# Seven products of quarter blocks in cross-attention's query and output projections

## The chip, the cores and the metric

The kernel runs on one core of a Trainium2 chip. The metric is the device time of one execution in microseconds (us); the median of the runs is what counts. A profiled execution gives the trace.

## What is computed

A decoder trunk of two layers over 256 tokens of width 1024, float32 throughout. Each layer mixes tokens, attends to 256 memory tokens, and applies a mixture of sixteen experts. The change is in the cross-attention:

```python
def memory_cross_attention(h, mem_n, wq, wkv, wo):
    q = (h @ wq).reshape(B, S, X_HEADS, X_DH)
    k, v = jnp.split(mem_n @ wkv, 2, axis=-1)
    ...
    s = jnp.einsum('bshd,bmhd->bhsm', q, k).astype(F32) * (X_DH ** -0.5)
    p = jax.nn.softmax(s, axis=-1)
    o = jnp.einsum('bhsm,bmhd->bshd', p, v.astype(F32)).reshape(B, S, D)
    return o.astype(h.dtype) @ wo

for l in range(DEPTH):
    ...
    x = x + jnp.concatenate([y_hg, y_att], axis=-1) @ w_out[l]
    x = x + memory_cross_attention(rms_norm(x, norm_cross[l]), rms_norm(mem, norm_mem[l]),
                                   wq_x[l], wkv_x[l], wo_x[l])
    x = x + hierarchical_moe(rms_norm(x, norm_ffn[l]), ...)
```

h is 256x1024, wq and wo are 1024x1024.

## The kernel before

**Engines and queues.** The kernel is written engine by engine, each engine's instructions in the order of the code, with semaphores between them. The sync engine (SP) only issues loads. TensorE does all products and transposes, VectorE and ScalarE empty PSUM and do the sums, maxima and exponentials, GpSimd does small roots and, in the token mixing, weight sums.

**Weights.** They come in units of 2 MB (128 partitions x 4096 floats, "ring" in the trace), each as two loads of 1 MB. The ring has six slots. `unit_places` deals units to slots in a fixed round: the layer's mixing units in the order of `UNITS` (o0 and o1: projection of the mixed tokens, q0 and q1: query projection, p0 and p1: output projection of cross-attention), a slot "sums" without a load, and then 48 expert units, six for each of eight pairs of experts: two gate, two up, two down. SP issues them in this order and waits before each until the slot's former tenant was used for the last time (`LAST_USE`, by the name of the job). In the last layer three more slots open for the experts, in buffers that have come free: `LATE`, `KEYS` and `WORK`, at the places of `LAST_SLOTS`.

**Banks.** Every product that goes to PSUM is a job with a name. `job_list` gives the order, and "A" or "D" says whether ScalarE or VectorE empties it; `bank_plan` deals the eight banks. TensorE opens a job when the bank's former job has been emptied (`open_bank`), and `wait_emptied` and `wait_job` are waits for the one or the other.

**Seven products.** The token mixing already computes two of its 256x1024x1024 projections together from seven products of quarter blocks (`seventh`, jobs m1 to m7, L617): the tokens are halved by rows and by columns, the weights likewise, and sums and differences of blocks are formed first. `rows_block(m, k)` is a quarter of the normed, transposed tokens hT (tokens m, columns k), `weight_block` half a unit, `token_sums(i)` a quarter of xs that holds a sum.

**Cross-attention before.** The products of the mixed tokens, wo00, wo10, wo01, wo11 (L710, closed by `rows_out`), are added to x by VectorE (L1577, in `add_rows`). Then for each tile m of 128 tokens ScalarE squares and sums x (L1034), GpSimd takes the root (L1225, L1226), VectorE scales x into xs (L1417), TensorE transposes xs (L508, jobs t3_m0 and t3_m1), and VectorE copies into hT with the gains (L1427). The query projection makes the queries transposed, weights stationary: qx0 in two halves of 128 tokens (L762), so that it can begin with the first tile, qx1 to qx3 over 256 tokens (L528 in `project_T`). ScalarE copies them to QxT (in "rot", L1056). `memory_scores` (L775) makes four jobs sx00, sx01, sx10, sx11, heads 2g and 2g+1 of tile m; VectorE takes maxima (L1589), ScalarE the exponentials (L1131), VectorE divides (L1597). The shares are transposed (pt jobs, L508), copied (L1602), and multiplied with the memory values (L791, jobs px0 to px3), which go back to hT. The output projection is four jobs ox00, ox10, ox01, ox11 of 128 tokens x 512 columns with the tokens stationary (L710), eight matmuls each, first half of the contraction first; VectorE adds them to x (L1577). Then come norm, transposes (t5 jobs), the router (L822) and the experts (L882 gate and up, L936 down).

Of the kernel before, what the change touches and what calls it, by code (L numbers as in the profile page):

```python
# [8 lines left out]
P = 128  # L9
# [7 lines left out]
D = 1024  # L17
# [21 lines left out]
LAST_SLOTS = {0: LATE, 5: KEYS, 6: WORK}  # L39
UNITS = ["k0", "k1", "v0", "v1", "hf", "hq", "hi", "av", "hg", "aq", "ak", "o0", "o1", "q0", "q1", "p0", "p1"]  # L40
SUMS = "sums"
# [10 lines left out]
def job_list():  # L52
# [15 lines left out]
    jobs += [(f"t3_{m}{c}", "D") for m, c in quarters]  # L68
    jobs += [(f"qx{k}", "A") for k in range(4)]
    jobs += [(f"sx{g}{m}", "A") for g in range(2) for m in range(M)]  # L70
    jobs += [(f"pt0{jb}", "D") for jb in range(2)] + [("px0", "D"), ("px1", "A")]
    jobs += [(f"pt1{jb}", "D") for jb in range(2)] + [("px2", "D"), ("px3", "A")]
    jobs += [(f"ox{n}{m}", "D") for m in range(M) for n in range(2)]
# [12 lines left out]
OPENED_AT = {"wo00": "et0", "wo10": "et0", "wo01": "et2", "wo11": "et2", "ox00": "px2", "ox10": "ox00", "ox01": "ox00", "ox11": "ox00"}  # L86


def bank_plan(more):
# [8 lines left out]
    for name in NAMES + more:  # L98
        for early, at in OPENED_AT.items():
            if at == name:  # L100
                begin(early)
        if name in more:
            free.sort(key=lambda bank: bank[0] in FIRST_ROWS)
        if name not in begun:
            begin(name)
        free.append((bank_of[name], name))
# [6 lines left out]
            "o0": "wo01", "o1": "wo11", "q0": "qx1", "q1": "qx3", "p0": "ox01", "p1": "ox11"}  # L113


def unit_places():
# [4 lines left out]
    for layer in range(DEPTH):  # L121
        units = UNITS[KV_UNITS if layer else 0:]
        at_sums = units.index("av") + 1
        order += [(layer, name, None) for name in units[:at_sums] + [SUMS] + units[at_sums:]]
# [4 lines left out]
    for layer, key, slot in order:  # L129
# [3 lines left out]
        places[layer, key] = slot, sum(k != SUMS for _, k in had) + 1, had[-1] if had else None  # L133
# [6 lines left out]
SCORES = [(0, (0, 2, 4, 6)), (0, (1, 3, 5, 7)), (1, (0, 2)), (1, (1, 3)), (1, (4, 6)), (1, (5, 7))]  # L140

# [42 lines left out]
def trunk(nc, x_in, mem_in, pos_in, inv_in, gains_in, og_in, w_mix, w_router, w_experts, nf_in, out):  # L184
    ctx = ExitStack()
    with ctx:
# [92 lines left out]
        token_sum, weight_sum = sem("token_sum"), sem("weight_sum")  # L279
        q_done = sem("q_done")  # L280
# [107 lines left out]
        def weight_block(L, name, k):  # L388
            return unit(name, L)[:, 4 * k:4 * k + 4, :]

# [97 lines left out]
        def _(pe):  # L488
# [79 lines left out]
            def layers_from(L, sums_read=None):  # L568
# [181 lines left out]
                w = unit("q0", L)  # L750
                for m in range(M):
# [3 lines left out]
                    if m == 0:  # L755
                        wait_unit(L, "q0")
                        b = open_bank(L, "qx0")
                    for k in range(2):
                        for c in range(C):
                            if k == 0 and c % 4 == 0:  # L760
                                wait_emptied(pe, L, f"t3_{m}{c // 4}")
                            last = nc.tensor.matmul(b[:, k * T + m * P:k * T + (m + 1) * P], w[:, c, k * P:(k + 1) * P],  # L762
                                                    hT[:, c, m * P:(m + 1) * P], start=(c == 0), stop=(c == C - 1))
                close(last)
                for k in range(1, 4):
                    wait_unit(L, f"q{k // 2}")
                    project_T(L, f"qx{k}", hT, unit(f"q{k // 2}", L), 2 * (k % 2))
                wait_emptied(pe, L, "qx3")
                def memory_scores(g):
                    for m in range(M):  # L770
                        b = open_bank(L, f"sx{g}{m}")
                        for i in range(2):
                            h = 2 * g + i
                            for k in range(2):
                                last = nc.tensor.matmul(b[:, i * T:(i + 1) * T], QxT[:, 2 * h + k, m * P:(m + 1) * P],  # L775
                                                        KT[:, 2 * h + k, :], start=(k == 0), stop=(k == 1))
# [1040 lines left out]
```

## Time and profile before

| | us |
|---|---|
| median of 3 runs | 1061.05 |
| lowest and highest | 1060.15, 1063.64 |
| span of the profiled execution | 1058.3 |
| TensorE busy in it | 1020.7 (96%) |
| VectorE busy | 413.4 (39%) |
| ScalarE busy | 135.6 (13%) |
| GpSimd busy | 98.2 (9%) |

The span reaches from the first to the last instruction of the profiled execution. Busy times are sums over the whole span; which engine is waited for in a stretch is read from the chain of waits and the timeline. A float32 matmul stands as two MATMUL rows in the trace, and its weight load as two LDWEIGHTS rows, which run beside matmuls. A row's mean duration is from its start to its modelled end, and rows overlap; the busy time divided by the count gives the distance at which they follow each other.

### The profile page before, as it was taken

How to read it: one execution, taken by the hardware profiler on the slowest of the kernel's cores; microseconds unless marked ns; L12 is line 12 of the kernel's file. 1: busy time of each engine (PE TensorE's matmuls, PEld its weight loads, DVE VectorE, ACT ScalarE, POOL GpSimd, SP SyncE). 2: the span in 40 equal slices, each digit the busy share in tenths (PEclk: the TensorE clock that was granted, in tenths of full speed). 3: DMA queues.
4: the chain of work that ended last, by engine and by line, in shares of the span. 5: the costliest groups of instructions: out<-in, count | busy, mean ns of one | idle time of the engine just before them, and what ended most of it. 6: DMA issues, size and time to landing. Idle time of an engine off the chain costs nothing.

```text
span 1058.3 us, 10640 instructions
## 1 busy us (share of the span) xinstructions
PE 1020.7 (96%) x4360; PEld 546.8 (52%) x4360; DVE 413.4 (39%) x734; ACT 135.6 (13%) x307; POOL 98.2 (9%) x123
## 2 busy tenths in 40 slices
PE   6999999999999999999999999999999999999996
PEld 6667556567564453333334855566864433333332
DVE  3433474622143324232334526572032534433333
ACT  2211001412010011110111000041011010011011
POOL 2051131000001000000000512200000100000000
PEclk9999999999999999999999999999999999999999
DMA  9944002954049999999999420088364699999994
GB/s 359 424 183 159 1 0 100 412 207 159 1 159 355 381 423 422 414 423 420 420 421 420 180 80 0 1 356 346 120 234 159 241 423 420 421 420 421 422 421 169
DMA packets 43671, 293.54 MB, mean 277 GB/s; under 512 B 5344, under 2 KB 5600, under 8 KB 10848
## 3 DMA queue, kind: packets, MB, share of 16 engines
q1 hardware_dynamic: 36848, 266.35, 61.8%
q10 hardware_dynamic: 5616, 22.24, 5.4%
q0 software_dynamic: 1152, 4.19, 1.0%
q8 instruction: 37, 0.61, 0.2%
q14 instruction: 18, 0.15, 0.0%
HBM read 283.33 MB, written 9.44 MB: 277 GB/s over the span
## 4 chain that ended last, share of the span: by engine, by line
PE 89%; DVE 3%; DMA 3%; ACT 2%; SPq 2%; issue 1%; POOL 0%; DVEq 0%; POOLq 0%; ACTq 0%
PE bank L882 19%; PE bank L710 10%; PE bank L936 10%; PE bank L528 9%; PE bank L518 8%; PE bank L546 5%; PE bank L548 5%; PE bank L941 5%; PE bank L617 5%; PE bank L639 3%; DMA ring<-in_w_experts 3%; PE bank L508 2%; SPq L469 2%; PE bank L762 1%; PE bank L775 1%; PE bank L791 1%
## 5 line engine op out<-in xcount | busy, mean ns | idle before, releaser
L882 PE MATMUL bank<-ring,hT 128*64 128x512 f32 x704 | 182.8, 594 | 0.5 <-DMA ring<-in_w_experts 0.5
L710 PE MATMUL bank<-ring,hT 128*128 128x512 f32 x256 | 112.1, 594 | 0.0
L882 PEld LDWEIGHTS bank<-ring,hT 128*64 128x64 f32 x704 | 57.8, 137 | 94.2 <-issue 92.8
L1721 DVE TENSOR_TENSOR x<-bank,x 128x512 f32<-128x512 f32 x64 | 44.3, 692 | 138.1 <-PE bank L941 138.1
L528 PE MATMUL bank<-hT,ring 128*128 128x256 f32 x448 | 97.4, 379 | 0.8 <-DVE hT L1427 0.8
L528 PEld LDWEIGHTS bank<-hT,ring 128*128 128x128 f32 x448 | 84.9, 190 | 12.8 <-issue 1.4
L518 PE MATMUL bank<-ring,hT 128*128 128x512 f32 x192 | 84.4, 592 | 0.0
L710 PEld LDWEIGHTS bank<-ring,hT 128*128 128x128 f32 x256 | 48.0, 190 | 57.7 <-issue 56.8
L936 PE MATMUL bank<-ring,Vx 128*64 128x512 f32 x208 | 58.3, 596 | 2.7 <-ACT Vx L1163 2.4
L941 PE MATMUL bank<-PT 128*128 128x512 f32 x128 | 59.2, 605 | 0.0
L936 PE MATMUL bank<-ring,work 128*64 128x512 f32 x256 | 56.7, 595 | 2.4 <-ACT work L1163 2.4
L518 PEld LDWEIGHTS bank<-ring,hT 128*128 128x128 f32 x192 | 35.6, 190 | 40.2 <-issue 40.2
L1221 POOL TENSOR_TENSOR sm<-sm 128x1 f32<-128x1 f32 x4 | 1.0, 239 | 474.5 <-ACT rot L1043 474.5
L941 PEld LDWEIGHTS bank<-PT 128*128 128x128 f32 x128 | 23.0, 189 | 36.0 <-issue 35.0
L936 PEld LDWEIGHTS bank<-ring,work 128*64 128x64 f32 x256 | 17.6, 137 | 36.3 <-issue 32.0
L882 PE MATMUL bank<-late,hT 128*64 128x512 f32 x80 | 35.3, 594 | 0.5 <-DMA late<-in_w_experts 0.5
L936 PEld LDWEIGHTS bank<-ring,Vx 128*64 128x64 f32 x208 | 18.2, 137 | 33.4 <-issue 26.6
L882 PE MATMUL bank<-work,hT 128*64 128x512 f32 x80 | 35.3, 594 | 0.0
L639 PEld LDWEIGHTS bank<-work 128*128 128x128 f32 x256 | 31.1, 192 | 7.7 <-issue 6.7
L1577 DVE TENSOR_TENSOR x<-bank,x 128x512 f32<-128x512 f32 x16 | 11.0, 690 | 59.5 <-PE bank L710 59.5
L1709 DVE TENSOR_SCALAR work<-work 128x512 f32<-128x512 f32 x8 | 3.4, 427 | 78.4 <-ACT work L1159 78.4
L1169 ACT ACTIVATE PT<-bank 128x512 f32<-128x512 f32 x32 | 19.1, 597 | 108.5 <-PE bank L936 108.5
(270 smaller groups left out, 1287.3 us busy)
## 6 DMA issues: line engine op xcount, KB each, us to landing
ring<-in_w_experts SPq DMA_DIRECT2D x160, 1024.0 KB, 14.3
ring<-in_w_mix SPq DMA_DIRECT2D x60, 1024.0 KB, 16.8
late<-in_w_experts SPq DMA_DIRECT2D x12, 1024.0 KB, 21.5
keys<-in_w_experts SPq DMA_DIRECT2D x10, 1024.0 KB, 21.0
work<-in_w_experts SPq DMA_DIRECT2D x10, 1024.0 KB, 24.8
late<-in_w_mix ACTq DMA_DIRECT2D x4, 2048.0 KB, 10.2
rot<-by_slot ACTq DMA_DIRECT2D x14, 512.0 KB, 8.2
by_slot<-late ACTq DMA_DIRECT2D x1, 4096.0 KB, 37.9
```

Source lines behind the costliest of these rows:

```text
L469: sp.dma_start(slot_view(slot)[:, half * n:(half + 1) * n], src[:, half * n:(half + 1) * n]).then_inc(loaded[slot][half], 16)
L518: last = nc.tensor.matmul(b[:, :], lhs[:, c, m * P:(m + 1) * P], w[:, c, :], start=(c == 0), stop=(c == C - 1))
L528: last = nc.tensor.matmul(b[:, k * T:(k + 1) * T], w[:, c, (n2 + k) * P:(n2 + k + 1) * P], rhs[:, c, :], start=(c == 0), stop=(c == C - 1))
L546: last = nc.tensor.matmul(b[:, k * T:(k + 1) * T], w[:, c, n:n + P], memory[:, c, :], start=(c == 0), stop=(c == C - 1))
L548: last = nc.tensor.matmul(b[:, :], memory[:, c, (j % 2) * P:(j % 2 + 1) * P], w[:, c, :], start=(c == 0), stop=(c == C - 1))
L617: last = nc.tensor.matmul(b[:, :], rows_at[:, c, :], weights[:, c, :], start=(c == 0), stop=(c == 3))
L639: last = nc.tensor.matmul(b[:, a * P:(a + 1) * P], K[:, a, m * P:(m + 1) * P], Q[:, a, m * P:(m + 1) * P], start=True, stop=True)
L710: last = nc.tensor.matmul(held[name[1:], n, m][:, :], hT[:, c, m * P:(m + 1) * P], w[:, c, :], start=(c == 0), stop=(c == C - 1))
L882: last = nc.tensor.matmul(banks[2 + g][b2 * CAP:(b2 + 1) * CAP, :], rows_T_of(p)[:, c, b2 * CAP:(b2 + 1) * CAP], w, start=(c == 0), stop=( ...
L936: last = nc.tensor.matmul(banks[5 + n][b2 * CAP:(b2 + 1) * CAP, :], ractT_of[L][:, c, b2 * CAP:(b2 + 1) * CAP], w, start=(c == 0), stop=(c ...
L941: routed_job(nc.tensor.matmul(banks[OUT_BANK[n][m]][:, :], gatedT[:, m, :], yrows[:, n * W:(n + 1) * W], start=True, stop=True))
L1721: V.tensor_tensor(xv, banks[OUT_BANK[n][m]][:, :], xv, ALU.add).then_inc(r_added[L], 1)
```

## The change

Both projections of cross-attention are computed from seven products of quarter blocks, as the token mixing's are.

- **Query projection.** `q_seventh` replaces L762 and the three jobs of L528. A product is 128 tokens x 512 query columns over 512 of the contraction: sixteen matmuls of 128 columns with the weights stationary. Their order is q_1, q_2, q_6, q_5, q_7, q_3, then two score jobs, then q_4, then two score jobs. Four of the seven products accumulate on a bank that already holds another product's sum (`ONTO`): q_6 on q_1, q_7 on q_6, q_4 on q_7, q_3 on q_5. The bank is read after each product that is part of a result, and the next product waits for that read. ScalarE copies q_1, q_6, q_5 and q_4 into QxT; VectorE adds q_2, q_7 and q_3 there. Results: block (tile 0, columns 1) is q_1 + q_2, (0, 0) is q_1 + q_6 and q_5 + q_3, and so on.
- **Output projection.** `p_seventh` replaces the four ox jobs: p_1, then the values of heads 2 and 3, then p_7, p_6, p_5, p_4, p_2, p_3, four matmuls of 512 columns each, with p_6 on p_1, p_4 on p_7 and p_3 on p_5. VectorE adds the banks into x, p_6's into three blocks.
- **Sums.** VectorE forms four weight sums of 128x2048 and four token sums of 128x512 for each projection. The weight sums stand in new slots of the ring (`Q_SUMS` after q1, `P_SUMS` after p1) and in place in the first halves of q0, q1, p0 and p1. VectorE waits for all of q0 and q1 before its first add into x, and for all of p0 and p1 after the add of q_2.
- **Slots.** The two new tenants move all later units by one or two slots; `LAST_SLOTS` opens the last layer's three slots one unit earlier. p1 now follows o0 in its slot.
- **Order of the scores.** Tile 1 of heads 0 and 1 comes first (`SX_ORDER`).

The diff, cut to its core:

```diff
-LAST_SLOTS = {0: LATE, 5: KEYS, 6: WORK}
+LAST_SLOTS = {0: LATE, 4: KEYS, 5: WORK}
...
+SUMS_AFTER = {"av": SUMS, "q1": Q_SUMS, "p1": P_SUMS}
...
+ONTO = {"q_6": "q_1", "q_7": "q_6", "q_4": "q_7", "q_3": "q_5", "p_6": "p_1", "p_4": "p_7", "p_3": "p_5"}
...
-            "o0": "wo01", "o1": "wo11", "q0": "qx1", "q1": "qx3", "p0": "ox01", "p1": "ox11"}
+            "o0": "wo01", "o1": "wo11", "q0": "q_3", "q1": "q_4", Q_SUMS: "q_4", "p0": "p_2", "p1": "p_3", P_SUMS: "p_4"}
...
+                def q_seventh(name):
+
+                    rows_at, sums_at, weights, weights_at = {
+                        "q_1": (rows_block(0, 0), 0, weight_block(L, "q1", 0), 0), "q_2": (rows_block(0, 1), 0, weight_block(L, "q1", 1), 0),
+                        "q_5": (token_sums(0), 1, weight_block(L, Q_SUMS, 0), 1), "q_6": (token_sums(1), 2, weight_block(L, Q_SUMS, 1), 2),
+                        "q_7": (token_sums(2), 3, weight_block(L, "q0", 0), 3), "q_3": (token_sums(3), 4, weight_block(L, "q0", 1), 0),
+                        "q_4": (rows_block(1, 1), 0, weight_block(L, "q1", 0), 4)}[name]
...
+                    if sums_at:
+                        pe.wait_ge(q_token_sum, 4 * L + sums_at)
+                    if weights_at:
+                        pe.wait_ge(q_weight_sum, 4 * L + weights_at)
+                    b = open_bank(L, name)
+                    for n in range(4):
+                        for c in range(4):
+                            last = nc.tensor.matmul(b[:, n * P:(n + 1) * P], weights[:, c, n * P:(n + 1) * P], rows_at[:, c, :],
+                                                    start=(name not in ONTO and n == 0 and c == 0), stop=(n == 3 and c == 3), skip_group_check=(name in ONTO))
+                    close(last)
...
+                memory_scores(0, 1, "q_7")
+                memory_scores(0, 0, "q_3")
+                q_seventh("q_4")
+                memory_scores(1, 0, "q_2")
+                memory_scores(1, 1, "q_4")
...
+                    b = open_bank(L, name)
+                    for c in range(4):
+                        last = nc.tensor.matmul(b[:, :], rows_at[:, c, :], weights[:, c, :], start=(name not in ONTO and c == 0),
+                                                stop=(c == 3), skip_group_check=(name in ONTO))
+                    close(last)
+
+                p_seventh("p_1")
+                memory_values(1)
+                for i in (7, 6, 5, 4, 2, 3):
+                    p_seventh(f"p_{i}")
...
+                q_weights(1, qt1, q12, q11)
+                q_weights(2, qt2, q22, qt1)
+                add_out(0, 0)
+                q_weights(3, q12, q22, q12)
+                add_out(1, 0)
...
+                q_sum("q_2", 0, 1, "q_1")
+                q_weights(4, q11, q21, qt2)
...
+                p_weights(1, pt1, p12, p11)
+                p_weights(2, pt2, p22, pt1)
+                p_weights(3, p12, p22, p12)
+                q_sum("q_7", 1, 0, "q_5")
+                q_sum("q_3", 0, 0, "q_6")
...
+                p_sum("p_1", (1, 0))
...
+                p_sum("p_7", (0, 1))
+                p_weights(4, p11, p21, pt2)
...
+                p_sum("p_6", (0, 1), (0, 0), (1, 1))
...
+                p_sum("p_5", (0, 1))
+                p_sum("p_4", (0, 0))
...
+                p_sum("p_2", (1, 0))
+                p_sum("p_3", (1, 1))
```

TensorE in layer 0, from the transposes of the second tile to the end of the scores, before (L508 transposes, L762 and L528 query projection, L775 scores; an x16 row is sixteen matmuls):

```order
L508 MATMUL bank3<-ident,xs 128x128 x4
L508 MATMUL bank4<-ident,xs 128x128 x4
L762 MATMUL bank5<-hT,ring 128x128 x16
L528 MATMUL bank6<-hT,ring 128x256 x16
L528 MATMUL bank1<-hT,ring 128x256 x16
L528 MATMUL bank2<-hT,ring 128x256 x16
L775 MATMUL bank7<-keys,rot 128x256 x4
L775 MATMUL bank0<-keys,rot 128x256 x4
L775 MATMUL bank3<-keys,rot 128x256 x4
L775 MATMUL bank4<-keys,rot 128x256 x4
```

and after (L785 is `q_seventh`, L803 the scores; a product whose tokens are named xs takes a token sum):

```order
L526 MATMUL bank4<-ident,xs 128x128 x4
L526 MATMUL bank5<-ident,xs 128x128 x4
L785 MATMUL bank6<-hT,ring 128x128 x16
L785 MATMUL bank3<-xs,ring 128x128 x16
L785 MATMUL bank1<-xs,ring 128x128 x16
L785 MATMUL bank3<-xs,ring 128x128 x16
L785 MATMUL bank1<-xs,ring 128x128 x16
L803 MATMUL bank2<-keys,rot 128x256 x4
L803 MATMUL bank7<-keys,rot 128x256 x4
L785 MATMUL bank3<-hT,ring 128x128 x16
L803 MATMUL bank0<-keys,rot 128x256 x4
L803 MATMUL bank4<-keys,rot 128x256 x4
```

All matmuls of the query projection now have 128 columns, and the last product stands between the score jobs.

VectorE in layer 0 from its copy of the first attention values to its last copy into hT, before (L1569 the copy, L1577 adds into x, L1417 the norm's scaling, L1427 copies into hT):

```order
L1569 COPY hT<-bank3 128x512
L1577 TENSOR_TENSOR x<-bank5,x 128x512
L1577 TENSOR_TENSOR x<-bank6,x 128x512
L1417 TENSOR_SCALAR xs<-x,sm 128x1024
L1577 TENSOR_TENSOR x<-bank1,x 128x512
L1577 TENSOR_TENSOR x<-bank2,x 128x512
L1427 TENSOR_TENSOR hT<-bank7,gains 128x4x128
L1427 TENSOR_TENSOR hT<-bank0,gains 128x4x128
L1417 TENSOR_SCALAR xs<-x,sm 128x1024
L1427 TENSOR_TENSOR hT<-bank3,gains 128x4x128
L1427 TENSOR_TENSOR hT<-bank4,gains 128x4x128
L1589 TENSOR_REDUCE sm<-bank7 128x2
```

and after, in two pieces, around the adds into x (L1617 the copy, L1626 weight sums, L1647 adds, L1465 scaling):

```order
L1617 COPY hT<-bank3 128x512
L1626 TENSOR_TENSOR ring<-ring 128x2048 x2
L1647 TENSOR_TENSOR x<-bank5,x 128x512
L1626 TENSOR_TENSOR ring<-ring 128x2048
L1647 TENSOR_TENSOR x<-bank6,x 128x512
L1465 TENSOR_SCALAR xs<-x,sm 128x1024
L1647 TENSOR_TENSOR x<-bank1,x 128x512
```

and between the last copy into hT and the first maximum (L1636 token sums, L1675 adds of q_2, q_7 and q_3, L1631 weight sums of the output projection):

```order
L1475 TENSOR_TENSOR hT<-bank5,gains 128x4x128
L1636 TENSOR_TENSOR xs<-hT 128x512
L1636 TENSOR_TENSOR xs<-xs,hT 128x512
L1636 TENSOR_TENSOR xs<-hT 128x512
L1636 TENSOR_TENSOR xs<-hT,xs 128x512
L1675 TENSOR_TENSOR rot<-bank6,rot 128x4x128
L1626 TENSOR_TENSOR ring<-ring 128x2048
L1631 TENSOR_TENSOR ring<-ring 128x2048 x3
L1675 TENSOR_TENSOR rot<-bank3,rot 128x4x128
L1675 TENSOR_TENSOR rot<-bank1,rot 128x4x128
L1692 TENSOR_REDUCE sm<-bank2 128x2
```

Three weight sums now stand before and between the first adds, four token sums and four more weight sums between the last copy into hT and the first maximum.

## Rows read from the trace of the kernel before

**Rows 1.** The execution's span and mean granted clock.

```profile
core 0: 1058.3 us, clock 0.999
```

**Rows 2.** The span in 40 slices: granted clock and DMA, in tenths.

```profile
PEclk9999999999999999999999999999999999999999
DMA  9944002954049999999999420088364699999994
```

**Rows 3.** The chain of waits: start us, length us, what.

```profile
223.51 3.81 PE bank L762 x32
...
228.53 3.84 PE bank L762 x32
232.37 20.74 PE bank L528 x96
253.78 7.19 PE bank L775 x32
...
263.13 3.72 PE bank L791 x16
...
267.73 3.53 PE bank L710 x8
...
274.71 24.05 PE bank L710 x56
298.78 0.70 DVE x L1577
...
736.43 3.81 PE bank L762 x32
...
830.09 13.98 PE bank L882 x64
...
1014.87 27.22 DMA ring<-in_w_experts
```

**Rows 4.** Sync queue issues; one stretch: engines busy, clock, DMA share, GB/s.

```profile
177.21 8.09 SPq L469 DMA_DIRECT2D ring<-in_w_mix  x12
...
837.27 0.80 SPq L469 DMA_DIRECT2D late<-in_w_experts  x2
...
837.20:1042.10 204.90, 199.75 (x874) 72.51 (x870) 81.01 (x116) 20.98 (x38) 0.00 (x0) 1.00 1.00 416
```

**Rows 5.** L762 by form: count | busy us, mean ns; TensorE waits.

```profile
L762 PE MATMUL bank<-hT,ring 128*128 128x128 f32 x128 | 15.3, 278 | 2.1 <-DVE hT L1427 2.1
...
L762 PEld LDWEIGHTS bank<-hT,ring 128*128 128x128 f32 x128 | 14.6, 192 | 3.0 <-issue 1.9 <-DVE hT L1427 1.2
...
PE bank L762 <- DVE hT L1427: 2.1, 4, 0.7
...
PE bank L775 <- ACT rot L1056: 1.4, 2, 0.7
```

**Rows 6.** Sums on VectorE and GpSimd by form: count | busy us, mean ns.

```profile
L1545 DVE TENSOR_TENSOR work<-bank,bias 128x256 f32<-128x256 f32 x8 | 3.3, 417 | 0.0
...
L1439 DVE TENSOR_TENSOR xs<-hT 128x512 f32<-128x512 f32 x4 | 2.8, 692 | 0.1
...
L1261 POOL TENSOR_TENSOR ring<-ring 128x2048 f32<-128x2048 f32 x2 | 9.0, 4508 | 32.4 <-DMA ring<-in_w_mix 32.4
```

**Rows 7.** Timeline around layer 0's first adds into x: start us, length us.

```profile
206.71 0.69 DVE L1569 COPY hT<-bank 128x512 f32<-128x512 f32 x1 [1.24 <-PE bank L701]
...
215.07 0.69 DVE L1577 TENSOR_TENSOR x<-bank,x 128x512 f32<-128x512 f32 x1 [2.74 <-PE bank L710]
...
217.97 0.75 DVE L1417 TENSOR_SCALAR xs<-x,sm 128x1024 f32<-128x1024 f32 x1 [2.20 <-POOL sm L1226]
...
221.74 1.04 PE L508 MATMUL bank<-ident,xs 128*128 128x128 f32 x8
```

**Rows 8.** Timeline of VectorE and GpSimd in layer 0's first token sums.

```profile
70.99 4.89 DVE L1439 TENSOR_TENSOR xs<-xs,hT 128x512 f32<-128x512 f32 x1
...
70.40 4.93 POOL L1265 TENSOR_TENSOR ring<-ring 128x2048 f32<-128x2048 f32 x1
```

More of the change, by code:

```diff
@@ L67, in job_list @@
     jobs += [(f"wo{n}{m}", "D") for m in range(M) for n in range(2)]
-    jobs += [(f"t3_{m}{c}", "D") for m, c in quarters]
-    jobs += [(f"qx{k}", "A") for k in range(4)]
-    jobs += [(f"sx{g}{m}", "A") for g in range(2) for m in range(M)]
+    jobs += [("t3_00", "D"), ("t3_01", "D"), ("q_1", "A"), ("t3_10", "D"), ("t3_11", "D"), ("q_2", "D"), ("q_6", "A"), ("q_5", "A"), ("q_7", "D"), ("q_3", "D"), ("sx01", "A"), ("sx00", "A"),
+             ("q_4", "A"), ("sx10", "A"), ("sx11", "A")]
     jobs += [(f"pt0{jb}", "D") for jb in range(2)] + [("px0", "D"), ("px1", "A")]
-    jobs += [(f"pt1{jb}", "D") for jb in range(2)] + [("px2", "D"), ("px3", "A")]
-    jobs += [(f"ox{n}{m}", "D") for m in range(M) for n in range(2)]
+    jobs += [(f"pt1{jb}", "D") for jb in range(2)] + [("p_1", "D"), ("px2", "D"), ("px3", "A")]
+    jobs += [(f"p_{i}", "D") for i in (7, 6, 5, 4, 2, 3)]
     jobs += [(f"t5_{m}{c}", "D") for m, c in quarters]
@@ L85 @@
 FIRST_ROWS = (0, 1)
-OPENED_AT = {"wo00": "et0", "wo10": "et0", "wo01": "et2", "wo11": "et2", "ox00": "px2", "ox10": "ox00", "ox01": "ox00", "ox11": "ox00"}
+OPENED_AT = {"wo00": "et0", "wo10": "et0", "wo01": "et2", "wo11": "et2"}
+ONTO = {"q_6": "q_1", "q_7": "q_6", "q_4": "q_7", "q_3": "q_5", "p_6": "p_1", "p_4": "p_7", "p_3": "p_5"}
 def bank_plan(more):
@@ L103, in bank_plan @@
             free.sort(key=lambda bank: bank[0] in FIRST_ROWS)
-        if name not in begun:
+        if name in ONTO:
+            bank_of[name], before[name] = bank_of[ONTO[name]], ONTO[name]
+        elif name not in begun:
             begin(name)
-        free.append((bank_of[name], name))
+        if name not in ONTO.values():
+            free.append((bank_of[name], name))
     return bank_of, before
@@ L122, in unit_places @@
         units = UNITS[KV_UNITS if layer else 0:]
-        at_sums = units.index("av") + 1
-        order += [(layer, name, None) for name in units[:at_sums] + [SUMS] + units[at_sums:]]
+        for name in units:
+            order.append((layer, name, None))
+            if name in SUMS_AFTER:
+                order.append((layer, SUMS_AFTER[name], None))
         more = LAST_SLOTS if layer == DEPTH - 1 else {}
@@ L132, in unit_places @@
         had = tenants.setdefault(slot, [])
-        places[layer, key] = slot, sum(k != SUMS for _, k in had) + 1, had[-1] if had else None
+        places[layer, key] = slot, sum(k not in ALL_SUMS for _, k in had) + 1, had[-1] if had else None
         had.append((layer, key))
@@ L754, in layers_from, with memory_scores @@
                         transposes(L, f"t3_{m}{c2}", by_columns(xs, m, c2))
[L755 to L776, printed above, removed]
-                        close(last)
+                    q_seventh(f"q_{m + 1}")
+                for i in (6, 5, 7, 3):
+                    q_seventh(f"q_{i}")
+                def memory_scores(g, m, ready):
+                    wait_emptied(pe, L, ready)
+                    b = open_bank(L, f"sx{g}{m}")
+                    for i in range(2):
+                        h = 2 * g + i
+                        for k in range(2):
+                            last = nc.tensor.matmul(b[:, i * T:(i + 1) * T], QxT[:, 2 * h + k, m * P:(m + 1) * P],
+                                                    KT[:, 2 * h + k, :], start=(k == 0), stop=(k == 1))
+                    close(last)
                 def memory_weights(g):
```

152 lines of the change are left out of this document (110 added, 42 removed).

## The prediction

> **What bounds the kernel now.** First the span and the granted clock: one core, 1058.3 us, clock 0.999 [rows 1]. The median of the runs shown is 1061.05 us, so 2.75 us lie outside the span; I carry them unchanged and make the sum against the span. Then the slices [rows 2]: the granted clock is at its top level throughout (in tenths, 9 everywhere), so no term here is a clock term, and the DMA engines are full in two stretches, the expert phases, and nearly idle between them. Then the chain of waits [rows 3]. Through layer 0's cross-attention it is TensorE nearly without a break: L762 and L528 (query projection), L775 (scores), L791 (values), L710 (output projection). Layer 1 repeats it 512.92 us later (736.43 against 223.51). The last 44 us are different: 27.22 us of a load of expert weights, then a little TensorE.
>
> So what does a gain in cross-attention do to the end? Layer 0's experts are TensorE's work, and it starts earlier by the gain. In layer 1 the tail is the weight stream: from 837.2 to 1042.1 us the DMA engines are 1.00 busy at 416 GB/s [rows 4]. 39 units of 2.10 MB at that rate are 197 us, the rest are rows of tokens. The stretch starts when the sync queue can issue the first unit whose slot pair 0's gate products free: issued at 837.27, after the chain's gate products that begin at 830.09 [rows 3, 4]. Nine of the 48 expert units are loaded before that point, 39 after. The change moves more units into the ring, but LAST_SLOTS keeps it at nine: of layer 1's units, (1, 3) is still the first that waits for (0, 0). The stream thus starts earlier by whatever TensorE gains, and its length stays. A gain in either layer therefore reaches the end whole, unless one of the cases below holds.
>
> **The change, part by part, per layer.** A matmul of this kernel stands as two in the trace, so sixteen in the order are 32 rows. *Query projection, products.* Before: 64 rows of 128 columns, 3.81 + 3.84 us, and 96 rows of 256 columns, 20.74 us [rows 3], 28.39 us. After: seven products of sixteen matmuls of 128 columns, 224 rows. The 128-column pitch is 15.3 us / 128 = 0.1195 us [rows 5], 26.77 us. Gain 1.62 us: less than an eighth of the work, because 128 columns cost 0.1195 where half of a 256-column row is 0.108.
>
> *Query projection, waits.* Before, TensorE stood still 2.1 us at L762 and 1.4 us at L775 over both layers [rows 5]. The first train of L762 ends at 227.32, eight transpose rows take 0.88 us (266.85 to 267.73 in the chain), and the second starts at 228.53 [rows 3]: 0.33 us a layer is a wait for VectorE's copy of these transposes. In their place q_2 reads tokens copied earlier, and has no such wait. L775's 0.70 us a layer is the wait for the last projection's copy; the first scores now read products that were summed earlier. Gain 1.03 us, if the covers below hold. Laying the new order out from 223.51 us with the pitches above, q_1 ends at 227.3, q_2 at 232.0, q_6 235.8, q_5 239.6, q_7 243.5, q_3 247.3, two score tiles (7.19 / 4 = 1.80 each) 250.9, q_4 254.7, two more tiles 258.3. The values follow 2.16 us after the last score tile before (260.97 to 263.13) [rows 3], and still do: 260.5 instead of 263.13.
>
> *VectorE's new sums.* Eight weight sums of 128x2048 a layer. VectorE has no such row; bounds are its 128x512 row with both inputs in SBUF, 0.692 us, times four, 2.77 us, and GpSimd's 128x2048 row, 4.508 us [rows 6]; from below, the slope between 128x256 (0.417) and 128x512 is 0.275 us for 256 elements, so 0.692 + 6 x 0.275 = 2.34 us. I take 2.36 with its wait, the slope being VectorE's own. Eight token sums cost 0.73 each. Where each falls:
> - Three weight sums before and between the first adds into x. VectorE is free from about 207.4 (after the copy at 206.71); two sums end at 212.1, the add of wo00 (ready one product of 3.44 us before wo10) at 212.8, the third at 215.2, the add of wo10 starts at 215.2 against 215.07 now. The normed tile is then ready at about 218.9 and TensorE wants it at 221.74 [rows 7]. Cover 2.8 us; free. They need q0 and q1 loaded: six units are issued from 177.21, and at the 416 GB/s of the long stretch a unit of 2.10 MB takes 5.0 us [rows 4], so q1, fourth in line, lands at about 199. Layer 1 the same.
> - Four token sums after the last hT tile, 229.1 to 232.0. q_6 wants the second, at 230.6, at 232.0. Free.
> - Weight sum 4 and the three p sums, 232.8 to 242.3; then the add of q_7 (243.5), wanted at 247.3. Free with 3.0 us to spare. q_3's add ends 1.0 us before sx00 wants it, q_4's copy on ScalarE 1.1 us before sx11 does.
> - In the output part: token sums 2 and 3 wait for px3's copy, 272.7, and end at 274.2; p_6 wants the third at 275.4. The last weight sum, 276.2 to 278.6, is wanted by p_4 at 282.3. Free.
>
> *Output projection.* Before 64 rows of 512 columns: 3.53 + 24.05 = 27.58 us [rows 3], 0.43 each. After 56 rows: 24.13. Gain 3.44 us. p_1 waits for px0 and px1 as ox00 did. The tail is unchanged: tile 0's last add is p_4's, two products before the end as ox10's was, so the first norm has its squares, root and scale under p_2 and p_3; the second norm begins after p_3 as it did after ox11 (DVE at 298.78).
>
> *Loads.* p1 now waits for wo01; in layer 1 it holds the sync queue, and the first expert unit behind it, until about 731 (wo01 ends 3.4 us after wo10, 218.5 in layer 0); it lands at about 737, wanted at about 748. The last three units before gate 0 are issued in the last 4 us of the projection (p_2's unit and p_3's two) and need 15 us; gate 0 starts 18 us after its end (811.7 to 830.09). Free.
>
> *GpSimd's port.* Elsewhere the trace shows what a GpSimd sum does to VectorE: a 128x512 sum took 4.89 us instead of 0.69 beside a 4.93 us sum of GpSimd [rows 8]. In this stretch GpSimd has only the roots of the norms, and VectorE stands at a wait for each of them, so neither holds the other. Nothing counted.
>
> Sum per layer: 1.62 + 1.03 + 3.44 = 6.1 us; two layers 12.2 us. 1061.05 - 12.2 = **1048.8 us**.
>
> **Rivals.**
> - *The pace of 128 columns is the weight load's.* A load of 128x128 weights lasts 192 ns against the pitch of 119.5 [rows 5]. If 16 products in a row wore out the overlap, the query part would cost 224 x 0.192 = 43.0 us, 14.6 more than now: per layer 14.6 - 1.03 - 3.44 = 10.1 us slower, 1081 us. Against it: the 128 rows of L762 run in long trains of 32 at 119.5. Chance 0.02. The Trainium skill (TensorE: Matmul & The Clock Gate, "The mechanism") has a rule that points to this rival: a weight load runs beside matmuls only if it goes to another group of rows of the array. With its price for a load of 128 columns, 107 ns, set before each row of 0.108 us, an estimate by that page is 224 x 0.215 = 48.2 us for the query part. By that rule the trace disagrees: rows that fill all 128 rows of the array already follow at 119.5 ns, less than one load lasts.
> - *VectorE becomes the bound (the one that ends slower).* At a price d for a 128x2048 sum, the first norm is late by 3d - 9.5 us and q_7's add by 4d - 13.7 us, where these are positive. At GpSimd's 4.5 us that is 4.0 + 4.3 = 8.3 us lost against 6.1 won: 2.2 us slower a layer, 1065.5 us. It costs from d = 3.2 on and decides from d = 4.2. For it: GpSimd's row. Against: VectorE's 0.692 us. Chance 0.04.
> - *The weight stream hides layer 1's gain.* If the stream did not start earlier (a unit less before gate 0, or late landings), one layer's 6.1 us would be lost: 1054.9 us. For it: the chain's 27.22 us of DMA. Against: the stream starts with a release by TensorE. One unit of 2 MB fewer is 5.0 us, nearly the same. Chance 0.07.
> - *The change doesn't save what it says:* the covers of 1.0 and 1.1 us (q_3, q_4) and the waits at the banks shared by two products fail by about 1 us each: 1051 us. Chance 0.12.
>
> **How the numbers follow.** Forecast 0.75, with 1047.5 to 1050.5 of its own; the last rival 0.12, the stream 0.07, VectorE 0.04, the pace 0.02. From below, the shorter gaps between longer trains may give 1 us more. The range, 1047.0 to 1055.5, takes in all but the two slow rivals and odd cases. A measurement of this kernel can tell about 0.3%, 3.2 us, from no change: 1057.9 to 1064.2 is "the same". Faster 0.91, same 0.03, slower 0.06.
>
> **What would show it.** In the profile after: the query products' rows at a pitch of 119 to 121 ns, 224 a layer; no idle time before the scores' rows; VectorE's 128x2048 rows at 2.3 us; 56 rows of 512 columns in the output projection without a gap; layer 1's first gate product at about 818 instead of 830.09; the weight stream starting at about 825 and still some 205 us long. Wrong if the 128-column pitch is above 0.13, if a VectorE weight sum takes over 3.2 us, if TensorE stands before the score tiles, or if the stream still starts where it did.

## The result, and the profile after

The changed kernel takes 1044.31 us, the median of 4 runs (1044.12 to 1045.82), against 1061.58 us for the kernel before in 4 runs beside it (1060.15 to 1063.64): a ratio of 0.983, with a 95% interval of 0.981 to 0.985. It is faster, as predicted, but by 17.3 us, not 12.2; 1044.3 lies below the range of 1047.0 to 1055.5. The profiled executions say nearly the same, 16.4 us: a span of 1041.9 us against 1058.3, at a mean granted clock of 0.998 against 0.999.

```profile
core 0: 1041.9 us, clock 0.998
```

```profile
PEclk9999999999999999999999999999999999999999
DMA  9954001844169999999999520074385899999994
```

As in [rows 2], the clock is at its top level throughout, and the DMA engines are full in the two expert phases. The chain of waits through layer 0's cross-attention, and its end (start us, length us, what), which answers to [rows 3]:

```profile
223.19 3.81 PE bank L785 x32
227.00 0.87 PE bank L526 x8
227.87 17.87 PE bank L785 x160
245.74 3.46 PE bank L803 x16
249.19 3.57 PE bank L785 x32
252.76 3.47 PE bank L803 x16
...
258.40 3.72 PE bank L819 x16
...
263.01 3.67 PE bank L849 x8
...
270.13 20.61 PE bank L849 x48
290.77 0.70 DVE x L1732
...
814.32 13.98 PE bank L929 x64
...
998.35 27.32 DMA ring<-in_w_experts
```

L785 is the query product, L526 the transposes, L803 the scores, L819 the values, L849 the output product, L1732 the last add into x, L929 an expert's gate product; the last row is the load of the last expert weights. From the first query row to the end of the scores TensorE has no gap (the six rows add up to 33.05 of 33.04 us); before it had 1.00 us of them. By stretches, in us:

| stretch, layer 0 | before | after | gained | predicted |
|---|---|---|---|---|
| start of the last train of wo to the first query row | 15.54 | 15.36 | 0.18 | 0 |
| first query row to the end of the scores | 37.46 | 33.04 | 4.42 | 2.65 |
| end of the scores to the first value row | 2.16 | 2.17 | 0 | 0 |
| first value row to the last add into x | 35.65 | 32.37 | 3.28 | 3.44 |
| sum | 90.81 | 82.94 | 7.87 | 6.1 |

The last row, twice, is 15.7 us, and layer 1's first gate product moves from 830.09 to 814.32, by 15.77. The weight stream, one window, against [rows 4]:

```profile
821.50:1025.70 204.20, 199.29 (x874) 72.15 (x870) 80.97 (x116) 20.93 (x38) 0.00 (x0) 1.00 1.01 416
```

Its first load is issued at 821.49, 15.78 us earlier than the 837.27 of before, and it is 204.2 us long instead of 204.9. The two profiles then differ by 16.4 us; the 0.9 us that the medians differ by beyond that most likely lie in how executions start (below); only profiled executions show that. The query rows by form, the new sums of VectorE, and what TensorE still waits for (count | busy us, mean ns | idle; then us in total, times, longest):

```profile
L785 PE MATMUL bank<-xs,ring 128*128 128x128 f32 x256 | 28.9, 275 | 0.0
...
L1631 DVE TENSOR_TENSOR ring<-ring 128x2048 f32<-128x2048 f32 x8 | 18.3, 2289 | 0.2
L1626 DVE TENSOR_TENSOR ring<-ring 128x2048 f32<-128x2048 f32 x8 | 18.3, 2283 | 0.1
L803 PE MATMUL bank<-keys,rot 128*128 128x256 f32 x64 | 14.5, 379 | 0.0
...
PE bank L819 <- DVE PT L1705: 2.6, 2, 1.3
```

28.9 / 256 is 0.113 us a row where the prediction had 0.1195. The sums cost VectorE 2.28 us (predicted 2.34 before its wait). L775's wait of [rows 5] has gone, L803 has none.

### The profile page after: what moved, and what is told of

It reads as the page before. It is cut to its first block, busy times and chain, and to the rows that moved or that the text cites. A ratio compares the mean times of both kernels' runs of the same rounds, so it can differ in the third digit from the quotient of the medians.

```text
span 1041.9 us, 10960 instructions
## 1 busy us (share of the span) xinstructions
PE 1006.3 (97%) x4472; PEld 543.1 (52%) x4472; DVE 470.3 (45%) x782; ACT 135.7 (13%) x307; POOL 98.5 (9%) x123
## 4 chain that ended last, share of the span: by engine, by line
PE 89%; DVE 3%; DMA 3%; SPq 1%; ACT 1%; issue 1%; POOL 0%; DVEq 0%; POOLq 0%; ACTq 0%
PE bank L929 19%; PE bank L983 10%; PE bank L536 8%; PE bank L564 5%; PE bank L728 5%; PE bank L546 5%; PE bank L566 5%; PE bank L988 5%; PE bank L785 5%; PE bank L849 5%; PE bank L635 5%; PE bank L657 3%; DMA ring<-in_w_experts 3%; PE bank L526 2%; SPq L487 1%; PE bank L819 1%
## 5 line engine op out<-in xcount | busy, mean ns | idle before, releaser
L929 PE MATMUL bank<-ring,hT 128*64 128x512 f32 x752 | 196.6, 594 | 0.2 <-DMA ring<-in_w_experts 0.2
L929 PEld LDWEIGHTS bank<-ring,hT 128*64 128x64 f32 x752 | 62.3, 137 | 108.2 <-issue 107.0
L1856 DVE TENSOR_TENSOR x<-bank,x 128x512 f32<-128x512 f32 x64 | 44.3, 692 | 137.7 <-PE bank L988 137.7
L536 PE MATMUL bank<-ring,hT 128*128 128x512 f32 x192 | 84.4, 592 | 0.0
L536 PEld LDWEIGHTS bank<-ring,hT 128*128 128x128 f32 x192 | 35.6, 190 | 40.2 <-issue 40.2
L546 PE MATMUL bank<-hT,ring 128*128 128x256 f32 x256 | 55.7, 379 | 0.8 <-DVE hT L1475 0.8
L728 PE MATMUL bank<-ring,hT 128*128 128x512 f32 x128 | 56.3, 596 | 0.0
L546 PEld LDWEIGHTS bank<-hT,ring 128*128 128x128 f32 x256 | 48.6, 190 | 8.0 <-issue 1.4
L728 PEld LDWEIGHTS bank<-ring,hT 128*128 128x128 f32 x128 | 23.8, 190 | 28.7 <-issue 28.1
L983 PE MATMUL bank<-ring,Vx 128*64 128x512 f32 x160 | 36.5, 596 | 2.0 <-ACT Vx L1211 1.7
L929 PE MATMUL bank<-late,hT 128*64 128x512 f32 x80 | 35.3, 594 | 0.5 <-DMA late<-in_w_experts 0.5
L1331 POOL TENSOR_TENSOR work<-work 128x256 f32<-128x256 f32 x28 | 20.6, 735 | 121.1 <-PE bank L657 121.0
L657 PE MATMUL bank<-work 128*128 128x128 f32 x256 | 31.2, 275 | 0.0
L1475 DVE TENSOR_TENSOR hT<-bank,gains 128x512 f32<-128x512 f32 x24 | 15.3, 683 | 34.1 <-PE bank L526 34.1
```

Source lines behind the costliest of these rows:

```text
L536: last = nc.tensor.matmul(b[:, :], lhs[:, c, m * P:(m + 1) * P], w[:, c, :], start=(c == 0), stop=(c == C - 1))
L546: last = nc.tensor.matmul(b[:, k * T:(k + 1) * T], w[:, c, (n2 + k) * P:(n2 + k + 1) * P], rhs[:, c, :], start=(c == 0), stop=(c == C - 1))
L657: last = nc.tensor.matmul(b[:, a * P:(a + 1) * P], K[:, a, m * P:(m + 1) * P], Q[:, a, m * P:(m + 1) * P], start=True, stop=True)
L728: last = nc.tensor.matmul(held[name[1:], n, m][:, :], hT[:, c, m * P:(m + 1) * P], w[:, c, :], start=(c == 0), stop=(c == C - 1))
L929: last = nc.tensor.matmul(banks[2 + g][b2 * CAP:(b2 + 1) * CAP, :], rows_T_of(p)[:, c, b2 * CAP:(b2 + 1) * CAP], w, start=(c == 0), stop=( ...
L983: last = nc.tensor.matmul(banks[5 + n][b2 * CAP:(b2 + 1) * CAP, :], ractT_of[L][:, c, b2 * CAP:(b2 + 1) * CAP], w, start=(c == 0), stop=(c ...
```

## What the extra gain could be

The prediction missed 1.8 us a layer between the first query row and the values. Two readings stand against each other.

**A, the train.** The chain shows how rows of 128 columns follow each other when nothing breaks the train: 17.87 / 160 = 0.1117 us. A train of 32 that starts after a pause lasts 3.81 = 0.347 + 31 x 0.1117: its first row counts with its whole length (the longest of the query rows in the profile is 0.348 us, the middle one 0.275), 0.24 us more than a row inside a train; the train of 32 that follows the scores directly lasts 3.57 = 32 x 0.1117. All four trains of [rows 5] start after a pause, so 15.3 / 128 = 0.1195 holds a quarter of a microsecond of restart in every 32 rows. By A the change gains 28.39 - (3.81 + 17.87 + 3.57) = 3.14 us in the query products, and 0.26 more because the scores no longer start after a pause (7.19 against 3.46 + 3.47).

**B, the wait.** The 128-column row does cost 0.1195 us, or as much more as its weight load (192 ns) shows through, and the gain beyond 2.65 us comes from elsewhere in the change: a wait or a contention that the profile of before does not name, or the output projection.

## The experiments

Times of whole executions also differ by how they start: the first load of the memory tokens and the first train of TensorE vary by 2 to 3 us between executions of one kernel. Two chain rows, of the changed kernel's profile and of a repeat of it, show where TensorE's second train begins:

```profile
39.67 27.47 PE bank L566 x64
```

```profile
42.56 27.47 PE bank L566 x64
```

Besides the times the table therefore gives the profiled span less the start of this row ("rest"), in us; before it is 1018.5, and three profiles of the changed kernel give 1002.2, 1002.3 and 1002.5.

| run | median us (runs) | ratio, 95% interval | rest | against after's 1002.2 |
|---|---|---|---|---|
| e1 query part only | 1052.44 (4) | 0.992 [0.990, 0.993] | 1009.1 | +6.9 |
| e2 output part only | 1055.39 (4) | 0.994 [0.993, 0.996] | 1011.1 | +8.9 |
| e3 before, short rows | 1061.89 (10) | 1.000 [0.999, 1.002] | 1019.6 | (before +1.1) |
| e4 doubled sums | 1075.10 (4) | 1.011 [1.009, 1.014] | 1031.0 | +28.8 |
| e5 a slot less | 1050.73 (4) | 0.990 [0.988, 0.992] | 1007.6 | +5.3 |
| e6 after again | 1046.43 (5) | 0.986 [0.984, 0.987] | 1002.3 | +0.1 |
| e7 shares early | 1043.67 (5) | 0.983 [0.981, 0.984] | 999.3 | -2.9 |
| e8 wait first | 1046.31 (1) | | 1002.3 | +0.1 |
| e9 one sum more | 1045.80 (5) | 0.984 [0.982, 0.985] | 1002.7 | +0.4 |
| e10 two sums more | 1049.19 (6) | 0.988 [0.986, 0.990] | 1006.3 | +4.1 |
| e11 after, third time | 1046.57 (4) | 0.984 [0.982, 0.986] | 1002.5 | +0.3 |

### The halves of the change: e1 and e2

e1 keeps the query part alone, e2 the output part alone, each cut out of the changed kernel. From e1's edit:

```diff
-LAST_SLOTS = {0: LATE, 4: KEYS, 5: WORK}
+LAST_SLOTS = {0: LATE, 5: KEYS, 6: WORK}
...
-SUMS_AFTER = {"av": SUMS, "q1": Q_SUMS, "p1": P_SUMS}
...
+SUMS_AFTER = {"av": SUMS, "q1": Q_SUMS}
...
-                p_seventh("p_1")
...
+                for n, m in outputs:
+                    close(rows_out("pox", n, m, range(4, C)))
```

> The query projection by seven products, the output projection as before. Theory A (the prediction's pitch was too high: the steady distance of 128-column rows is 0.1117 us, and a train that stands alone shows its last row's full length besides, so fewer breaks are worth more): 4.4 us a layer in the stretch from the first query product to the last maximum, and 0.15 us from the copies that now stand ahead of a wait, 9.1 us in all, ratio 0.9914. Theory B (the prediction's 0.1195 us and waits as counted): 2.65 us a layer, 5.3 us in all, ratio 0.9950. Theory C (the gain comes from the output projection or from the two together): under 5 us, and less than the whole minus the other half.

> The output projection by seven products, the query projection as before. All theories but C: eight rows of 512 columns fewer a layer, 3.3 to 3.4 us, 6.6 to 6.9 us in all, ratio 0.9936. Theory A with the sum: the gains of this kernel and of the one with the query part alone add up to the whole change's 17.3 us less about 1 us. Theory C: over 8 us here.

Against before the rest shrinks by 9.4 us in e1 and by 7.4 in e2, 16.8 together where the whole change has 16.3, so nothing of note comes from the two together. The predicted shares were 5.3 and 6.9 us. Up to layer 1's first gate product, before the weight stream has a part in it, the gains are 9.2 us in e1, 6.7 in e2 and 15.6 in the whole change (its start again counted from TensorE's second train). The miss is in the query part. e1's chain has the same rows as the whole change's:

```profile
223.41 3.81 PE bank L785 x32
227.22 0.87 PE bank L526 x8
228.09 17.87 PE bank L785 x160
```

This speaks for A, and rules the output projection out as a source.

### The pace alone: e3

The kernel before, with qx1 to qx3 as twice as many rows of 128 columns; the work and the order of all else are the same.

```diff
-                    project_T(L, f"qx{k}", hT, unit(f"q{k // 2}", L), 2 * (k % 2))
+                    project_T_short(L, f"qx{k}", hT, unit(f"q{k // 2}", L), 2 * (k % 2))
...
+                for m in range(M):
+                    for k in range(2):
+                        for c in range(C):
+                            last = nc.tensor.matmul(b[:, k * T + m * P:k * T + (m + 1) * P], w[:, c, (n2 + k) * P:(n2 + k + 1) * P],
+                                                    rhs[:, c, m * P:(m + 1) * P], start=(c == 0), stop=(c == C - 1))
```

> The kernel before, with the 96 rows of 256 columns of the query projection (qx1 to qx3) issued as 192 rows of 128 columns in one unbroken train, weights loaded twice; nothing else differs. Theory A: 192 x 0.1117 = 21.45 us in place of 20.74, 0.7 us a layer slower, 1.4 us in all, ratio 1.0013. Theory B: 192 x 0.1195 = 22.94 us, 2.2 us a layer, 4.4 us in all, ratio 1.0042. The rival by the weight load's 0.192 us: 36.9 us, 16 us a layer, 32 us in all, ratio 1.030.

The train, where before had `20.74 PE bank L528 x96` [rows 3], and the loads in it (both layers):

```profile
232.65 21.45 PE bank L539 x192
```

```profile
L539 PE MATMUL bank<-hT,ring 128*128 128x128 f32 x384 | 43.2, 275 | 0.0
L539 PEld LDWEIGHTS bank<-hT,ring 128*128 128x128 f32 x384 | 43.0, 192 | 0.0
```

21.45 / 192 = 0.1117 us, in a kernel that has nothing else of the change: 0.71 us a layer more than 96 rows of 256 columns, where 0.1195 would have made it 2.2. The rest grew by 1.1 us, the ratio is 1.000. B's pace falls. So does the prediction's rival of the weight load: 192 loads of 192 ns each stand in the 21.45 us, and the rows don't slow to the loads' length. The 0.71 us, 3.7 ns for each row of 128 columns, is all that twice as many rows and loads cost; no run tells the two apart. The Trainium skill (TensorE: Matmul & The Clock Gate, "Step-by-step: what each phase is for") says that in a stream the drain of one matmul hides behind the next and that only a lone one pays for it; by that rule, the trace agrees: 0.24 us more for a row after a pause, none inside a train.

### VectorE's covers: e9, e10 and e4

A cover is the time by which VectorE has something ready before TensorE wants it. e9 puts one more weight sum ahead of the three before the first adds into x, e10 two, and e4 doubles seven of the eight weight sums of a layer. The added sums change no result: each is overwritten by a later sum, or (two of e4's) forms again what stands there already.

```diff
+                more_weights(qt1, q12, q11)
                 q_weights(1, qt1, q12, q11)
+                more_weights(qt2, q22, qt1)
                 q_weights(2, qt2, q22, qt1)
```

The first line is e9, both are e10; e4 has such a line ahead of seven `q_weights` and `p_weights`.

> One more weight sum of 128x2048 (2.3 us; its result is overwritten) ahead of the three that stand before the first adds into x, in both layers. Cover theory (the prediction's): in the changed kernel the first normed tile is ready at 218.65 and TensorE wants it at 221.76, and the add of wo10 has some 0.3 us between it and the sum before; 2.3 us more on VectorE still fit. Time as the changed kernel of the same call, within 0.5 us; no wait for VectorE's L1465 before TensorE's L526. Rival (VectorE's chain is already the bound there, the three sums cost time): 2.3 us more a layer, 4.6 us.

> Two more such sums, 4.6 us a layer. Cover theory: the cover of about 3.1 us is overrun by 1.3 to 1.5 us (the run with three more showed a wait of 3.7 us for 6.9 us of sums, a cover of 3.2): 2.6 to 3.0 us slower than the changed kernel of the same call. The granted clock: the run with all sums doubled showed it at its lower level after waits of 3.7 and 6 us of TensorE. If it falls after a wait of 1.4 us too, the next transposes and the train of q_1 last longer (up to 0.87 and 3.57 us more), and the loss is up to 6 us more over two layers; if it does not fall, these show 0.87 and 3.81 us as ever.

> The changed kernel with seven of VectorE's eight weight sums a layer preceded by one more of the same size (their results are overwritten or not used), 4.6 us for a pair. The prediction's formula at d = 4.61, with the cover of q_7's add 1.5 us shorter because the products are faster: 4.3 + 6.2 = 10.5 us a layer against the changed kernel; laid out on its timeline 4.1 us late at q_1 and 6.0 us at the first score tile, 10.1 us a layer. So about 1064.5 us, ratio to the kernel before 1.003. If VectorE's sums have more cover than counted: less, down to 1044.3 us.

e9, with 2.3 us more work a layer on VectorE in the chain's neighbourhood, takes 1045.8 us against 1046.57 of e11 beside it: the cover is there. In e10 it is overrun. Its chain, and TensorE's waits:

```profile
217.23 2.29 DVE ring L1630
219.55 0.70 DVE x L1651
220.27 1.16 ACT rot L1081 x2
222.44 0.77 DVE xs L1465
223.25 1.09 PE bank L526 x8
224.34 0.75 issue
225.09 3.81 PE bank L785 x32
```

```profile
PE bank L526 <- DVE xs L1465: 3.5, 4, 1.3
```

The chain now goes through VectorE's sums, and TensorE stands 1.3 us. A layer loses 1.34, the restart of the transposes (1.09 against 0.87) and 0.2 before q_1, 1.75 us; the median is 2.6 us above e11's and the rest 3.8, where 2.6 to 3.0 was expected without the restarts. In this profile the trains after the wait are at the old pace. But two of e10's six executions took 1053.0 and 1053.1 us with a mean granted clock of 0.995; the profiled one took 1048.3 at 0.998, and no execution of e9 or of the changed kernel shows less than 0.998. A mean lower by 0.003 is about 3 us of full clock over the span. So the same waits may or may not bring the clock down; where it fell in these two executions no profile shows.

e4 was expected at 1064.5 us, as two overrun covers, and took 1075.1. Its waits are as large as thought:

```profile
PE bank L803 <- DVE rot L1682: 12.1, 2, 6.1
PE bank L526 <- DVE xs L1465: 8.2, 4, 3.7
```

What is left is slower trains, and most of that is the clock. Windows of e4 (stretch, then busy us of TensorE, its loads, VectorE, ScalarE, GpSimd with counts; granted clock, DMA share, GB/s), behind the wait of 3.7 us and around that of 6 us in layer 0, then behind the wait of 3.7 us in layer 1, and chain rows with trains behind the waits:

```profile
228.00:230.00 2.00, 2.00 (x10) 1.65 (x9) 1.83 (x4) 1.15 (x2) 0.00 (x0) 0.50 0.00 0
...
254.00:256.00 2.00, 0.00 (x0) 0.00 (x0) 1.97 (x2) 0.00 (x0) 0.00 (x0) 0.68 0.77 254
256.00:258.00 2.00, 0.00 (x0) 0.00 (x0) 1.97 (x2) 0.00 (x0) 0.00 (x0) 0.50 1.00 422
258.00:260.00 2.00, 1.39 (x3) 1.17 (x4) 1.15 (x2) 0.00 (x0) 0.00 (x0) 0.50 0.76 320
260.00:262.00 2.00, 2.00 (x7) 1.63 (x6) 0.00 (x0) 0.00 (x0) 0.00 (x0) 0.61 0.00 0
...
744.00:746.00 2.00, 0.86 (x8) 0.86 (x8) 1.67 (x3) 0.00 (x0) 0.22 (x1) 1.00 1.01 426
746.00:748.00 2.00, 1.25 (x8) 1.05 (x6) 1.47 (x3) 1.15 (x2) 0.31 (x2) 0.56 1.01 426
...
750.00:752.00 2.00, 2.00 (x11) 2.00 (x11) 0.00 (x0) 0.00 (x0) 0.00 (x0) 0.50 0.00 0
```

```profile
227.56 1.97 PE bank L526 x8
229.53 4.42 PE bank L785 x32
...
258.61 5.16 PE bank L803 x16
...
745.14 1.09 PE bank L526 x8
...
746.98 6.72 PE bank L785 x32
...
778.58 6.28 PE bank L803 x16
```

TensorE stood from 252.7 to 258.6; the granted clock fell to its lower level, 1.2 GHz, while it stood, was still there when the scores began, and came back to 2.4 GHz within the window that ends at 262. In layer 1, behind a wait as long as layer 0's (3.7 us), the transposes still ran at 1.00 (1.09 us, as in e10), and the clock fell only then, ahead of q_1's train. Against the rows of the changed kernel (0.87, 3.81, 3.46) these trains are longer by 1.10 + 0.61 + 1.70 us in layer 0 and 0.22 + 2.91 + 2.82 in layer 1, 9.4 us; about 1 us of it is the restarts of four trains (0.22 to 0.26 each), the other 8.4 the lower clock. Waits (12.1 + 8.2, less the 0.8 that the changed kernel has) 19.5, slower trains 9.4: 28.9, against 28.8 us by which the rest grew. So a late VectorE costs its lateness and, with waits as long as e4's, nearly half as much again.

### The tail: e5

One slot fewer for the experts of the last layer: eight units before the first gate product instead of nine.

```diff
-LAST_SLOTS = {0: LATE, 4: KEYS, 5: WORK}
+LAST_SLOTS = {0: LATE, 4: KEYS}
```

> The changed kernel with two more slots in the last layer in place of three (WORK is not used): eight expert units are loaded before the first gate product frees a slot, not nine. Theory of the stream (the end is the weight stream's, which starts with that release): one unit of 2.10 MB at 420 GB/s more, 5.0 us slower than the changed kernel, 1049.3 us, ratio to before 0.9884. If TensorE set the end of the last layer: no difference, 0.983.

TensorE reaches the gate product at the same time as in the changed kernel (814.22 against 814.32), and the last load ends 5.2 us later. The rest grew by 5.3 us, the median by 4.3 against e6 beside it:

```profile
814.22 13.98 PE bank L929 x64
...
1003.57 27.30 DMA ring<-in_w_experts
```

The end is thus set by when the stream starts and by how many units are left in it, as the prediction had it. Since the first gate product frees the stream, layer 1's gain reaches the end; that it did is what e5 and the shift of 15.77 us show together.

### Order: e7 and e8, with e6 and e11 beside them

e7 puts the transposes of the first shares between the last two score jobs, so that TensorE has scores to work on while VectorE copies them. e8 takes back one small thing of the change: in it VectorE waits until its own last add into x is done ahead of its copies into hT, as before the change. Of the two pieces below the first is e7's; the second is e8's, ahead of the copies for the query projection, and e8 has the same edit once more ahead of the copies for the router.

```diff
-                memory_scores(1, 1, "q_4")
                 memory_weights(0)
+                memory_scores(1, 1, "q_4")
...
-                memory_max(1, 1)
                 memory_kept(0)
+                memory_max(1, 1)
```

```diff
-                rows_T("t3", 0, 8)
                 wait_emptied(dve, L, "wo11")
+                rows_T("t3", 0, 8)
```

> The changed kernel once more, beside the next one: 1044.3 us, ratio 0.983.

> The changed kernel with the transposes of the first shares (pt00, pt01) ahead of the last score job in place of behind it, and VectorE's copies of them ahead of its last maximum. TensorE stood 1.3 us a layer for these copies; the last score tile now covers them: 1.3 to 1.4 us a layer, 2.7 us in all faster than the changed kernel, 1041.6 us, ratio to before 0.981. If the second shares then come late (their chain now starts 0.9 us later against a start 1.4 us earlier): no gain.

> The changed kernel with VectorE's wait for its own last add into x back ahead of the copies into hT, as in the kernel before (two places a layer). From the last add into x to the first query product 1.57 us in place of 1.42, so 0.15 us a layer later there; the copies before the router are not on the chain. 0.3 us in all, to be seen in the trace, not in the time.

> The changed kernel once more, for the two runs beside it: 1044 to 1047 us, ratio 0.983 to 0.986. Executions of one kernel differ by 2 to 3 us by the first load of the memory tokens (3.65 or 6.0 us in the chain's first rows); if that is so, the profiled execution's span less that row is 1038.3 us in either case.

e7's chain goes from the scores to the values without a step of VectorE's between them:

```profile
252.90 1.73 PE bank L803 x8
254.63 0.87 PE bank L526 x8
255.51 1.73 PE bank L803 x8
257.23 3.45 PE bank L819 x16
```

The values start 4.33 us after the first of these rows instead of 5.64 (252.76 to 258.40), and lose their restart too (3.45 against 3.72): 1.6 us a layer. The median is 2.8 us below e6's beside it, the rest 3.0 below e6's. e7 is the fastest kernel here, 0.983 of before where e6, the changed kernel beside it, has 0.986.

In e8 the first query row starts 1.52 us after the start of the last add into x (224.02 to 225.54), against 1.39 in the changed kernel (221.80 to 223.19) and 1.57 before (221.94 to 223.51). So the place of this wait gives 0.13 of the 0.18 us a layer in the table above. It is too little for the time: e8's rest is 1002.3 like e6's.

e11's expectation was half wrong: its load of the memory tokens took 3.78 us, not one of the long ones, and yet its second train began at 41.72, since its first train took 29.66 us where others have 27.89. Executions differ by two things at the start, not by one; from the second train on they agree within 0.3 us. The first train is longer through its first 3.5 us: from 13 to 16 us its rows follow each other at four a microsecond where the first profile of the changed kernel has six to seven, in both at a granted clock of 1.00. What slows them stays open.

## Why the prediction was right in sign and too small

**The bound and the path: right.** TensorE was the chain through both layers and is; the tail's stream starts with TensorE's gate product and is 204.2 us long (predicted "some 205"); both layers' gains reach the end (15.77 us at the gate, 16.3 in the rest).

**The step that failed: "the 128-column pitch is 15.3 us / 128 = 0.1195 us".** The term was 1.62 us a layer and measured 3.14. Busy time over count, which the text under the table of times calls the distance of rows, is that only in a long train; here it held one restart of 0.24 us in 32 rows. Taking it for the pace of a train of 160 overcharged 224 rows by 0.0078 us each, 1.7 us, less one restart that the new train has. The restart could have been read in the chain of before: sixteen rows of L791 last 3.72 us behind a pause [rows 3] and 3.45 in the train, in the row

```profile
271.26 3.45 PE bank L791 x16
```

that [rows 3] leaves out. The e3 run shows the pace alone: 0.1117 us. The prediction did allow for "shorter gaps between longer trains", at 1 us for the whole kernel; it was 3.0. With 3.14 in place of 1.62 the same sum gives 1045.8 us, 0.15% from the result.

**The waits of the query part: right, and short by their restarts.** 1.03 us was counted for the two waits removed, and they are gone: of before's 37.46 us, all but 1.00 was rows (28.39, 7.19 and the transposes' 0.88). But a pause also lengthens the train behind it, and the scores lost 0.26 us with it. A wait on TensorE costs its length and a quarter of a microsecond.

**The output projection: right.** 3.44 predicted, 3.28 measured: 3.67 + 20.61 for 56 rows, the first eight with a restart of 0.24.

**VectorE's sums: right.** 2.28 us against 2.34, the slope of [rows 6] times length; the bound by GpSimd's row was far off. The cover before the first adds was put at 2.8 us and is 3.1 (the normed tile is ready at 218.65, TensorE comes at 221.76): it carries one more sum (e9) and not two (e10). Nothing shows the port of [rows 8] in this stretch. The rival that ends slower had its mechanism right and its price too low: e4 stands for a sum of twice 2.3 us, 4.6, where the rival's two terms give 4.3 + 4.7 us a layer and the waits were 3.7 + 6.1, but 4.7 us a layer of slower trains came on top, 4.2 of them the clock.

**Left out: the order of VectorE's copies.** 0.18 us a layer, in no term of the sum; e8 gives 0.13 of it.

**The stream.** The first gate product came at 814.32, predicted "about 818"; the loads were in time, and no wait for them appears at the query or output products.

Of the 5.1 us that were missed, 3.0 are the pitch, 0.5 the scores' restart, 0.4 the copies, less 0.3 in the output projection; about 0.6 are a stream shorter by 0.6 us, which lies within what the kernels here with nine units ahead show from the first gate product to the last load (211.3 to 212.0 us, before itself 212.0), and the remaining 0.9 most likely the starts of the executions. That one unit of the stream more or less costs 5 us is shown (e5); why the stream's length differs by half a microsecond is not.

## What to carry to other kernels

Read TensorE's pitch from a long unbroken train (length over count in the chain), not from busy time over count of short ones; then charge each pause its length and one restart, here 0.24 us. Splitting a product into rows of 128 columns costs little as long as the train stays whole, so a scheme that saves an eighth of the work keeps most of it (28.39 us became 25.25 in the query products, where a full eighth would be 3.55). And size VectorE's covers against the new, faster TensorE: what is free here with 3.1 us to spare is bound by two sums more, and a wait of 3.7 or 6 us was paid for once more in the clock.

## What the runs showed of the hardware that was not expected

- A row of 128 columns in float32 follows the last by 0.1117 us while its weight load lasts 0.192 us, over 192 rows in a row. By these durations the load of the next row starts before that of the last has ended.
- In e4's layer 0, after TensorE stood 3.7 us, the granted clock was 0.50 in the next 2 us that it worked, and after 6 us likewise. In layer 1, after the same 3.7 us, it was still 1.00 for the transposes and fell behind them. The trains behind this wait were longer by 1.7 us in layer 0 and by 3.1 in layer 1: where the clock falls against the work behind the wait differs from place to place.
- After 1.3 us (e10) it stayed at 1.00 in the profiled execution, but two of six executions had a lower mean clock, 0.995, and took 4.7 us more.
